# A hybrid mixer's convolution without GpSimd: three split projection blocks, and key products ahead of half of the last block

## What is computed

```python
def hybrid_mixer(n, w_in, conv_w, conv_b, ...):          # n: rms_norm(x), 256 x 1024
    proj = jnp.einsum('bld,dp->blp', n, w_in)             # 4608 conv, 2048 gate, 64 scalar columns
    conv_in, gates, scal = jnp.split(proj, [CONV_CH, CONV_CH + GATE_CH], axis=-1)
    c = jax.nn.silu(centred_dwconv(conv_in, conv_w, conv_b))   # 7 taps along the tokens, per channel
    q, k, v, xs, Bm, Cm = jnp.split(c, ...)               # 1024, 1024, 1024, 1024, 256, 256 channels
    q = l2_normalize(q) * (GDN_HEAD_DIM ** -0.5)
    k = l2_normalize(k)
    ...                                                   # g, beta, dt from scal
    o_fw = gated_delta_chunked(q, k, v, g_fw, sigmoid(b_f))    # and the same backwards
    y_fw = ssd_chunked(x_ssd, dt_fw, sA[0], Bm, Cm)            # and the same backwards
    ...
```

## Time and profile before

| | |
| --- | --- |
| median of three runs | 1266.28 us (1262.86 to 1268.41) |
| the profiled execution: its time, its span | 1264.27 us, 1262.5 us |
| its mean granted clock of TensorE | 0.961 |
| TensorE, matmuls | 1116.3 us, 88% of the span, 6155 instructions |
| VectorE | 665.4 us, 53%, 1093 |
| ScalarE | 430.2 us, 34%, 1041 |
| GpSimd | 281.5 us, 22%, 273 |
| granted clock in 40 slices of 31.6 us | 9 tenths or more in the first ten, 7 to 9 tenths behind them |
| chain that ended last | TensorE 58%, VectorE 16%, DMA 16%, ScalarE 5% |
| taps on VectorE, L2294 | 168 x 530 ns, 87.9 us |
| additions on GpSimd, L2888 | 48 x 757 ns, 36.4 us |
| gate products 128x512, L785 | 128 x 593 ns |

### The profile page before, as it was taken

How to read it: one execution, slowest core, us unless ns; L and a number is a source line. 1 busy time by engine, 2 the same in 40 slices (tenths; PEclk the granted TensorE clock), 3 DMA queues, 4 the chain that set the end, 5 groups by cost and what they waited for, 6 DMA issues and landing times.

```text
span 1262.5 us, 15564 instructions
## 1 busy us (share of the span) xinstructions
PE 1116.3 (88%) x6155; PEld 829.0 (66%) x6155; DVE 665.4 (53%) x1093; ACT 430.2 (34%) x1041; POOL 281.5 (22%) x273
## 2 busy tenths in 40 slices
PE   7999999999898765576779999999888999999987
PEld 6888765677676411131257897886677788788666
DVE  3755957333783400010063466677786255667875
ACT  4759542233653300000064403304325531320432
POOL 0322331330410100000022123142452113224250
PEclk9999999999899888788889999999998999999999
DMA  7433435787518999999993454353322535434310
GB/s 214 168 132 121 178 102 166 241 297 266 204 67 333 392 421 421 421 422 421 413 210 122 154 179 151 116 200 134 134 73 91 179 122 183 156 106 165 131 67 33
DMA packets 94682, 255.81 MB, mean 203 GB/s; under 512 B 9873, under 2 KB 16322, under 8 KB 82322
## 3 DMA queue, kind: packets, MB, share of 16 engines
q1 hardware_dynamic: 90844, 251.18, 54.3%
q0 software_dynamic: 1152, 3.06, 1.0%
q10 hardware_dynamic: 2614, 0.59, 0.3%
HBM read 251.96 MB, written 2.59 MB: 202 GB/s over the span
## 4 chain that ended last, share of the span: by engine, by line
PE 58%; DVE 16%; DMA 16%; ACT 5%; issue 2%; SPq 2%; POOL 1%; ACTq 0%; DVEq 0%; POOLq 0%
PE bank L785 54%; DMA ring<-in_w_gate_dram 6%; DVE ring_r L2189 4%; PE bank L794 3%; DVE acc L2294 3%; DMA bias<-in_w_up_dram 2%; DMA ring<-in_w_up_dram 2%; DMA ring<-in_w_down_dram 2%; SPq L705 2%; DMA ring<-in_w_ada_dram 1%; DMA ring<-in_w_out_dram 1%; ACT L1662 1%; DVE ring L2304 1%; ACT ring L1662 1%; ACT oa L1662 1%
## 5 line engine op out<-in xcount | busy, mean ns | idle before, releaser
L3004 POOL CAST w_hi_r<-ring 128x1024 fp32r<-128x1024 f32 x136 | 152.8, 1152 | 619.8 <-DMA ring<-in_w_in_dram 253.5
L2189 DVE TENSOR_TENSOR ring_r<-ring,w_hi_r 128x1024 fp32r<-128x1024 f32 x136 | 185.0, 1390 | 51.8 <-POOL w_hi_r L3004 51.8
L785 PE MATMUL bank<-ring_r,xT_hi 128*128 128x512 f32 (+2 forms) x448 | 172.4, 385 | 0.0
L785 PE MATMUL bank<-w_hi_r,xT_hi 128*128 128x512 f32 (+1 forms) x368 | 147.9, 402 | 6.6 <-DVE xT_r L2194 3.4
L785 PE MATMUL bank<-w_hi_r,xT_r 128*128 128x512 f32 (+1 forms) x368 | 141.6, 385 | 0.0
L785 PE MATMUL bank<-xT,ring 128*128 128x256 f32 x576 | 126.3, 380 | 0.0
L785 PEld LDWEIGHTS bank<-xT,ring 128*128 128x128 f32 x576 | 109.2, 190 | 15.2 <-issue 0.6
L2294 DVE SCALAR_TENSOR_TENSOR acc<-raw,cols,acc 128x256 f32<-128x256 f32 x168 | 87.9, 530 | 29.0 <-ACT acc L1662 23.8
L785 PE MATMUL bank<-ring,xsT 128*32 128x512 f32 x320 | 76.5, 772 | 21.5 <-DMA bias<-in_w_up_dram 7.9
L785 PEld LDWEIGHTS bank<-ring_r,xT_hi 128*128 128x128 f32 x448 | 85.3, 190 | 14.4
L785 PEld LDWEIGHTS bank<-w_hi_r,xT_hi 128*128 128x128 f32 x368 | 69.4, 189 | 31.8 <-issue 9.3
(11 more groups left out here) (403 smaller groups left out, 2198.4 us busy)
## 6 DMA issues: line engine op xcount, KB each, us to landing
ring<-in_w_in_dram SPq DMA_DIRECT2D x38, 2048.0 KB, 7.7
ring<-in_w_ada_dram SPq DMA_DIRECT2D x12, 2048.0 KB, 9.2
ring<-in_w_gate_dram SPq DMA_DIRECT2D x24, 1024.0 KB, 21.0
ring<-in_w_down_dram SPq DMA_DIRECT2D x20, 1024.0 KB, 26.4
ring<-in_w_out_dram SPq DMA_DIRECT2D x8, 2048.0 KB, 8.0
ring<-in_w_up_dram SPq DMA_DIRECT2D x16, 1024.0 KB, 26.3
bias<-in_w_up_dram SPq DMA_DIRECT2D x6, 1024.0 KB, 25.4
ring<-in_w_in_dram SPq DMA_DIRECT2D x4, 1024.0 KB, 12.9
```

The source lines that it names most:

```text
L785: return release(nc.tensor.matmul(o, lhsT, rhs, start=start, stop=stop))
L2189: tt(lo, raw_, hi.bitcast(F32), ALU.subtract).then_inc(lo_done.sem, lo_done.one("piece"))
L3004: nc.gpsimd.tensor_copy(hi, raw_).then_inc(hi_done.sem, hi_done.one("piece"))
```

## The change

- **Six taps of every tile on VectorE.** The GpSimd additions and ScalarE's scaled copies for them go. VectorE takes the tiles in pairs and alternates between the two tiles of a pair, so that each tap waits for the tap two instructions ahead (`tapped[n]`) instead of the one ahead. `scalar_inputs` and `scalar_steps` both stand ahead of pair 2, 3.
- **Three split blocks.** The weights of blocks 1, 3 and 5, and the normed input `xT`, are split in two fp32r parts each: ScalarE copies the high part (`conv_high`), VectorE subtracts it (`conv_low`). TensorE forms such a product as three fp32r products (`mm3`: high by high, high by low, low by high). `conv_high(0)` stands in ScalarE's list ahead of tile 0, the others behind the first tap of tiles 7 and 15; `conv_low` stands ahead of pairs 0, 8 and 16.
- **Three places for the weights.** The first eight blocks go through places 0, 1 and 4 of the ring instead of 0 and 1.
- **Order at the end.** TensorE does the first half of block 8 (B), then the key products and the first four transposed banks, then the second half of block 8 (C), then the gates. B's transposed bank is the last one, between the two last gate tiles. VectorE goes from tile 31 to the key products and the inversion, and taps tiles 32 to 35 behind it. The sums of squares 4 to 7 go from block 5 to ahead of block 6. On ScalarE, the DMA issues that load back half of the inverses stand ahead of gate tile 3,0 instead of behind it.

```diff
@@ -108,6 +108,10 @@
+CONV_SLOTS = (0, 1, RING - 1)
+CONV_BLOCKS = CONV_CH // COLW
+CT_FIRST = BT0
+CONV_SPLIT = (1, 3, 5)
@@ -204,7 +208,7 @@
-    slot = [n % 2 if n < n1 else FIRST_PLACES[n - n1] if n < n1 + len(FIRST_PLACES) else NEXT_PLACES[(n - n1 - len(FIRST_PLACES)) % len(NEXT_PLACES)]
+    slot = [CONV_SLOTS[n % 3] if n < CONV_BLOCKS - 1 else n % 2 if n < n1 else FIRST_PLACES[n - n1] if n < n1 + len(FIRST_PLACES) else NEXT_PLACES[(n - n1 - len(FIRST_PLACES)) % len(NEXT_PLACES)]
@@ -304,7 +307,11 @@
-            V, T1 = late_all[:].rearrange("p a n -> p (a n)")[:, 512:1536], late_all[:].rearrange("p a n -> p (a n)")[:, 1536:1792]
+            V, T1 = Uraw, ntmp[:, 1, 0:T]
@@ -498,8 +503,8 @@
-            + [(bnat, BT0, 0, 0)] \
-            + [(knat, KT0, t, q) for t in range(TT) for q in range(2)]
+            + [(knat, KT0, t, q) for t in range(TT) for q in range(2)] \
+            + [(bnat, BT0, 0, 0)]
@@ -641,9 +646,15 @@
-        def conv_mine(pool):
-            return [n for n in range(CT) if (n % 4 == 3 and n < CT - 1) == pool]
+        def conv_piece(s, i):
+            at = slot[CONV_SPLIT[s]]
+            low = ring_r[at][:] if at < RING - 1 else hq_r[:].rearrange("p a n -> p (a n)")
+            return [v.rearrange("p (k n) -> p k n", k=DK)[:, :, i * P:(i + 1) * P] for v in (ring[at][:], low, ring_r[2][:])]
@@ -840,7 +853,14 @@
-                        last = mm(bank[b][:, i * T:(i + 1) * T], w[:, k, c:c + P], xT[:, k, :], k == 0, k == DK - 1)
+                        if pair // 2 in CONV_SPLIT:
+                            s = CONV_SPLIT.index(pair // 2)
+                            if k == 0:
+                                pe.wait_ge(conv_lo.sem, conv_part(s, 2 * j + i))
+                            _, lo, hi = conv_piece(s, 2 * j + i)
+                            last = mm3(bank[b][:, i * T:(i + 1) * T], (hi[:, k], lo[:, k]), (xs_hi[:, k, :], xs_lo[:, k, :]), k == 0, k == DK - 1)
+                        else:
+                            last = mm(bank[b][:, i * T:(i + 1) * T], w[:, k, c:c + P], xT[:, k, :], k == 0, k == DK - 1)
@@ -857,17 +877,19 @@
+                if n == 6:
+                    for i in range(4, 8):
+                        norm_pair(i)
@@ -932,33 +957,39 @@
-            first_gate = take("w_in")
-            gate_tile(0, 0, first_gate)
             for h in range(GH):
                 kq_decay(h)
             for i in range(4):
                 nat_bank(i)
-            gate_tile(0, 1, first_gate)
-            block_read()
+            conv_block(CONV_BLOCKS - 1, first=False)
+            gate_block(0)
             gate_block(1)
-            for i in range(4, 9):
+            for i in range(4, 8):
                 nat_bank(i)
             gate_block(2)
-            for i in range(9, 13):
+            for i in range(8, 12):
                 nat_bank(i)
-            gate_block(3)
+            last_gate = take("w_in")
+            gate_tile(3, 0, last_gate)
+            nat_bank(12)
+            gate_tile(3, 1, last_gate)
+            block_read()
@@ -1722,8 +1750,24 @@
+            def conv_high(s):
+                act.wait_ge(landed[slot[CONV_SPLIT[s]]], arrived(CONV_SPLIT[s]))
+                if s:
+                    act.wait_ge(used, CONV_SPLIT[s - 1] + 1)
+                for p in range(4):
+                    raw_, _, hi = conv_piece(s, p)
+                    f(hi, raw_, ACT.Copy).then_inc(conv_hi.sem, conv_hi.one("part"))
+            act.wait_ge(front_dve.sem, front_dve.at("n7"))
+            for t in range(TT):
+                k = slice(t * DK // 2, (t + 1) * DK // 2)
+                act.wait_ge(front_act.sem, front_act.at("n5"))
+                f(xs_hi[:, k], xT[:, k], ACT.Copy).then_inc(conv_hi.sem, conv_hi.one("part"))
+            conv_high(0)
@@ -1731,25 +1775,23 @@
-                if n in conv_mine(True):
...
-                    for j in range(1, CONV_K):
-                        f(conv_products[:, j - 1], raw[:, i, j:j + T], ACT.Copy, scale=tap(n, j)
-                          ).then_inc(conv_prod.sem, conv_prod.one("tap"))
+                for s in range(1, len(CONV_SPLIT)):
+                    if n == 4 * (CONV_SPLIT[s] - 1) - 1:
+                        conv_high(s)
-                if n in (18, 22):
-                    inverse_norms(n - 18)
+                if n in (18, 23):
+                    inverse_norms(0 if n == 18 else 4)
@@ -1785,18 +1826,23 @@
             for i in range(4):
                 nat_copy(i)
-            gate_tile_out(0, 1)
+            for n in range(CT - 2, CT):
+                conv_tile(n)
+            gate_out(0)
             gate_out(1)
...
-            gate_tile_out(3, 0)
             act.wait_ge(inv_out, 32)
             for q in range(QN):
                 act.dma_start(Xc[q * SQ:(q + 1) * SQ, :, :, 1, :].rearrange("p h c n -> p (h c) n"), block_rows(inverses, 1, q)
                               ).then_inc(inv_back, 16)
+            gate_tile_out(3, 0)
+            for n in range(CT_FIRST, CT):
+                conv_silu(n)
+            nat_copy(12)
             gate_tile_out(3, 1)
@@ -2272,30 +2319,55 @@
+            def conv_low(s):
+                for i in range(4):
+                    raw_, lo, hi = conv_piece(s, i)
+                    dve.wait_ge(conv_hi.sem, conv_part(s, i))
+                    tt(lo, raw_, hi.bitcast(F32), ALU.subtract).then_inc(conv_lo.sem, conv_lo.one("part"))
...
-            for n in conv_mine(False):
-                if n == 1:
+            def conv_pair(two):
+                if 2 in two:
                     scalar_inputs()
-                if n == 2:
                     scalar_steps()
...
+                for s in range(len(CONV_SPLIT)):
+                    if 4 * (CONV_SPLIT[s] - 1) in two:
+                        conv_low(s)
...
                 for j in range(1, CONV_K):
-                    ins = stt(out=acc[:, n % 4, :], in0=raw[:, n % 4, j:j + T], scalar=tap(n, j), in1=acc[:, n % 4, :],
-                              op0=ALU.mult, op1=ALU.add)
-                    if j < CONV_K - 1:
-                        link(ins)
+                    for n in two:
+                        if j == 1:
+                            dve.wait_ge(conv_tap0.sem, n + 1)
+                        else:
+                            dve.wait_ge(dve_chain, tapped[n])
+                        ins = stt(out=acc[:, n % 4, :], in0=raw[n % 4][:, j:j + T], scalar=tap(n, j), in1=acc[:, n % 4, :],
+                                  op0=ALU.mult, op1=ALU.add)
...
+            for n in range(0, CT_FIRST, 2):
+                conv_pair((n, n + 1))
@@ -2351,6 +2423,8 @@
             last.then_inc(inv_dve.sem, inv_dve.one("V"))
+            for n in range(CT_FIRST, CT, 2):
+                conv_pair((n, n + 1))
@@ -2881,14 +2955,6 @@
-            for i, n in enumerate(conv_mine(True)):
-                pool.wait_ge(conv_tap0.sem, n + 1)
-                for j in range(1, CONV_K):
-                    pool.wait_ge(conv_prod.sem, i * (CONV_K - 1) + j)
-                    ins = nc.gpsimd.tensor_tensor(acc[:, n % 4, :], acc[:, n % 4, :], conv_products[:, j - 1], ALU.add)
...
```

More of the change, by code:

```diff
@@ L286, in hybrid_kernel @@
             xn = w_hi[0][:].rearrange("p (t d) -> p t d", t=TT)
+            xs_hi, xs_lo = (v[:].rearrange("p (k n) -> p k n", k=DK) for v in w_hi_r)
             scalT, fold = ntmp[:, 0, 0:T], ntmp[:, 1, 0:SCAL]
@@ L832, in conv_tiles @@
                 b = pair % 4
-                if pair >= 4:
+                if pair == CT // 2 - 1:
+                    pe.wait_ge(nat_out.sem, b + 1)
+                elif pair >= 4:
                     pe.wait_ge(conv_in.sem, 2 * (pair - 4) + 2)
@@ L858, in norm_pair, with conv_block @@
                 mm(bank[4 + i % 4][:, T:2 * T], TRI["ones"], nsq[i][:, T:2 * T]).then_inc(norm_pe.sem, 1)
-            for n in range(CONV_CH // COLW):
-                w = take("w_in")
+            def conv_block(n, first=True, second=True):
+                w = take("w_in") if first else ring[slot[n]][:].rearrange("p (k n) -> p k n", k=DK)
                 if n == 4:
@@ L864, in _ @@
                         norm_pair(i)
-                conv_tiles(2 * n, w, 0, other_columns if n == 0 else None)
+                if n == 6:
+                    for i in range(4, 8):
+                        norm_pair(i)
+                if first:
+                    conv_tiles(2 * n, w, 0, other_columns if n == 0 else None)
                 if n == 0:
                     scalar_halves()
-                if n == 5:
-                    for i in range(4, 8):
-                        norm_pair(i)
                 if n == 1:
@@ L883, in _ @@
                     last.then_inc(front_pe.sem, front_pe.one("rows"))
-                conv_tiles(2 * n + 1, w, 1, scalar_sums if n == 0 else None)
-                block_read()
+                if second:
+                    conv_tiles(2 * n + 1, w, 1, scalar_sums if n == 0 else None)
+                    block_read()
+            for n in range(CONV_BLOCKS - 1):
```

(4 more changed lines are left out.)

88 lines of the change are left out of this document (47 added, 41 removed).

## The result

The changed kernel takes 1269.68 us (median of 12 runs, 1267.77 to 1272.30), the kernel before 1266.23 (12 runs, 1262.86 to 1268.41). The ratio is 1.0030, with a 95% interval of 1.0021 to 1.0040: slower by 0.3%, within the 0.5% that the forecast took as its limit. Forecast were 1270.3, and 1260 to 1277. The profiled execution of after took 1270.07 (span 1268.0), 5.8 over that of before; mean granted clock 0.954 against 0.961.

What follows compares the result with a forecast made beforehand. Two paths, TensorE's list and the inversion, ended within 6 us; the later end counts. TensorE's savings and new stalls sum to +4.0 us, taking the profiled 1264.27 to 1268.3, the median to 1270.3; range 1260 to 1277.

Steps and rivals of the forecast that it cites:

- The g stall: TensorE waits near 35 us for g, held by ScalarE's and VectorE's new work, until 41.2: +5.8 us.
- The copy of tile 33: TensorE, done with 34 tiles at 140.2, waits for ScalarE's copy of tile 33: +3.0 us.
- the 1.7 at the fifth head: TensorE waits 1.7 us for the fifth head's key products, which start at 150.4.
- Bank B: TensorE's last transposed bank needs the SiLUs of tiles 32 to 35: a wait of 2.45 us.
- From the transposes to the next stage: TensorE's rest from 155.9 takes 71.1 us instead of 55.1; with a gap of 0.84 the next stage starts at 227.9.
- The inversion: It ends earlier on VectorE, about 200.5 instead of 212.0, with GpSimd's products ready before TensorE asks.
- The split blocks: On TensorE three fp32r products replace each float32 product in three blocks of 32: -7.3 us.
- the end of pair 9: TensorE's work from g through pair 9 ends at 90.6 us, against 89.9 before.
- Removing the g wait alone gives only -2.8: Without TensorE's wait for g the gain is only 2.8 us, since VectorE then bounds the rest.
- rival A: Faster: g comes in time and TensorE's key products never wait; -6.5 us, 1259.8; chance 0.17.
- B: Slower: VectorE's taps stay at 0.52, the gap being its own; stage 4.0 + 11.2 late, 1281.5 us; chance 0.13.
- C: A little slower: blocks 3 and 5 wait for VectorE's parts; one late pair costs 4.8 us, 1275; chance 0.10.

Runs made afterwards that it cites:

- 12 fill products: Changed kernel with 12 extra unread products of xT by xT on TensorE during the wait for g: 1267.6 us, 1.0012 of the kernel before.
- sz early: Changed kernel with VectorE's two operations that make sz moved ahead of the first taps, behind block 1's second low part: 1263.0 us, 0.9980 of the kernel before.
- tile 19: As sz early, with ScalarE's copy of tile 19 also moved ahead of the first group of inverse norms: 1263.6 us, 0.9979 of the kernel before.
- without a split: Changed kernel with blocks 1, 3 and 5 as single float32 products, no high or low parts: 1271.2 us, 1.0043 of the kernel before.
- 24 fill products: Changed kernel with 24 extra unread products of xT by xT on TensorE ahead of g: 1274.5 us, 1.0069 of the kernel before.
- late inversion: Changed kernel with VectorE filling V ten more times behind the load of the blocks: 1278.0 us, 1.0094 of the kernel before.

## Why the prediction was right

**The sign and the size** came out, 1269.7 for 1270.3, and most of the ledger's lines with them:

- The g stall: forecast until 41.2, measured 40.82, 5.69 long for 5.8. The chain was the one named: high parts, two tiles, twelve taps, sz at 34.4 for 35.0, ScalarE's tables until 39.9.
- The copy of tile 33: 2.77 for 3.0. Behind it the clock was low (2.74 from the first head to the second, for 1.37); that took the place of the 1.7 at the fifth head, which is not there.
- Bank B: 1.91 for 2.45.
- From the transposes to the next stage: 71.4 for 71.9 (the 71.1 with the gap of 0.84); bank B makes the difference.
- The inversion: V stored at 203.1 for 200.5, products early, as forecast; and the second row block's weights, issued later, landed later. The next stage at 229.3 for 227.9.

**What was mis-sized.** The split blocks give 6.9, not 7.3: the pitch within them is 0.120, not 0.1185. The larger one is the stall for g, where only idle time was counted: the low clock behind it is 2.4 more, as the run with 12 fill products shows. The prediction gave the clock no term, because the kernel before has 9 tenths or more in its first ten slices; but the stall was new, so the slices of before could not show its price. Low clock and smaller saving, less 0.4 for the earlier g, carry the end of pair 9 from 90.6 to 92.9. From there 2.0 reach the transposes (157.9 for 155.9), and 0.6 less behind them puts the stage at 229.3 for 227.9.

**What was luck.** The fourth tile started at 25.71 instead of 26.29. By distance the front is 6.0 longer, where the forecast has 4.0: -6.9 split, +5.7 and +2.4 at g, +2.8 and +1.5 at the key products, +1.9 at bank B, -1.2 for the norm wait, -0.2 small. The profiled pair differs by 5.8 as well (1270.07, where 1268.3 was forecast for it). Only the medians differ by 3.5, which makes the forecast of the whole look 0.6 us good; no run explains that difference.

**What was wrong.** "Removing the g wait alone gives only -2.8, since VectorE then bounds the rest." In the run with sz early all three engines move, and 8.3 come back. The trace of after shows the room for it: VectorE's 8.92 idle ahead of tile 19 ends with ScalarE's norms, and ScalarE waits 3.70 for TensorE's bank ahead of them. The prediction gives no working for the 2.8; perhaps it held the queues of ScalarE and VectorE where the late sz had put them. Both stalls that rival A doubted are real; one small move takes the first away, a second one (tile 19) a third of the other, 2.74 to 1.83, and the one behind it, 1.37, whole. The remaining 1.83 is the price of the new order at the end, and none of the runs takes it away.

**The rivals.** A: the stalls are there. B: taps at 0.395. The statement of the Trainium skill ("VectorE: DVE Perf Modes", "The DRAIN you can't avoid"), made there from copies, that "the semaphore costs nothing extra here", does not fit these taps: with the wait on the one just ahead 0.52, without it 0.395. The same section also says that a next operation that is not held starts earlier, which the prediction left out and the 0.395 agrees with. C: blocks 3 and 5 had no stall, their rows stand without a gap.

**Left open.** The profiled pair differs by 5.8, the medians by 3.5; and the whole of the runs without a split, with 24 fill products and with the late inversion is 3 to 5 above what their fronts say. Why the low clock follows some short waits and not others is open too.

## What to carry to other kernels

An idle stretch of TensorE can have two prices, the wait and a low clock behind it; allow for both when new work is put ahead of a small operation that another engine's chain starts from, and put that small operation as early as its input allows. A saving on one engine is worth nothing in front of a wait that another sets: look at the first wait downstream before taking the edit. Two paths that end within a few us of each other must be shortened together.

## What was not expected of the hardware

- Products that nobody reads, in a wait of 5.7 us, shortened the front by 2.7 us (2.1 by the medians of the whole), since the granted clock stayed at 1.00 instead of 0.50.
- A wait of 1.87 us was followed once by 20 us at 0.50, in another run of the same program part (sz early) by none at all, and its next wait of 3.54 by some 5 us. Ahead of the key products the wait of 2.74 to 2.77 was followed by low clock in three runs (after, 12 fill products, late inversion) and not in two (sz early, 24 fill products).
- Two dependent taps of 128x256, one instruction of the other tile between them, start 0.395 us apart; with a wait on the one just ahead, 0.52, though each takes 0.48 in both.
